# A two-block transformer kernel on one Trainium2 core: another start (idle TensorE multiplies ones, two load queues, high products first) and another order of VectorE's work in a recurrence

## The chip, the cores and the metric

The kernel runs on one core of one Trainium2 chip. The metric is the device time of one execution in microseconds (us); for the kernel before it is the median of three runs. A core has a matmul engine (TensorE, PE in the rows), a vector engine (VectorE, DVE), a scalar engine (ScalarE, ACT), a general engine (GpSimd, POOL) and SyncE (SP), which here only issues transfers. Each has a program of its own, and they meet at semaphores.

## The reference, cut to what matters

The input is 256 tokens of width 1024. Two transformer blocks are computed one after the other. The part that the change touches is the first block's beginning:

```python
h = _rmsnorm(x, norm_mix_g[l])            # x * rsqrt(mean(x^2)) * gain
z = h @ w_in[l]                           # 1024 -> hq, hf, hi, hg, fq, fk, fv, ff, mq, gates
f = lb + (1.0 - lb) * sigmoid(f_logit)    # hf
qh, kh = silu(q), 1.0 - f                 # hq
G = cumsum(log(f))                        # within a chunk of 64 tokens
A[t,s] = sum_c q[t,c] k[s,c] exp(G[t,c] - G[s,c])      # s <= t
o = A @ i + (q * exp(G)) @ S              # S is carried from chunk to chunk
```

After this recurrence come forgetting attention, attention into a memory, a gated merge, a convolutional GLU, and a second block with two SwiGLUs and differential and dilated attention.

## The kernel before

**Weights.** All weights are cut into units of up to 128 x 2048 f32 (1 MB), loaded one after the other by SP into three `raw` buffers: unit i (`load(i)`, L2023) is issued when unit i-3 has been used up (`w_lo`). Each unit is split into a high and a low part in f32r: ACT copies `raw` to `wh` (`hi_to`, L848, "high"), which may overwrite the buffer of unit i-3 only when its products are done (`unit_end`), and DVE makes `wl = raw - wh` (`lo_to`, L1245, "low"). The activations are split in the same way into `hTh` and `hTl`. A product is then three matmuls for each of eight 128-row slices: high by high, high by low, low by high (`three`, L334; all its matmuls are recorded at L340). A unit of 256 columns takes 48 matmuls of 256 columns. Units come in the order hf (0, 1), hq (2, 3), hg (4, 5), ff (6, a small one), hi (7, 8), gate (9 to 20) and so on; the number is `U[key]`. `begin(key)` on ACT or DVE is `hi_to` or `lo_to` up to two units past that key.

**The start.** x comes turned (channels on partitions) in four pieces of 128 x 512 (`XT`), interleaved on SP's queue with four pieces of unit 0, then unit 1 in two halves, units 2 and 3, then x by tokens (`X`), constants (`C`) and small tables. The norm gains `GT` (128 x 48) come on ACT's queue (L906). For each piece ACT makes the high part of x times gain (L892) and of the weights (L915), DVE the low parts (L1359, L1366), and PE then does that piece's 24 matmuls (L433), waiting for the low parts ahead of all three products. The norm itself is applied later: ACT sums the squares of `X` (L880), DVE makes the reciprocal root and writes it onto a diagonal (`norm_end`, L1299), PE multiplies ones by that diagonal after the products of hq 0 (`spread(0)`, L396, called at L452), and DVE copies the outcome to `RB` and scales hf, hq and the others with it.

**The recurrence.** DVE makes f, k and the cumulated logs G. Seven levels (half sizes 1 to 64) of decays follow: `level_sub(n)` (DVE), exponential (ACT, L962), `level_mul(n)` (DVE), `level_products(n)` (PE, L486, matmuls at L493), `level_out(n)` (DVE). They are interleaved by hand with the 12 gate units: in iteration u PE does the products of gate u and then those of level u-1; DVE does `lo_to`, scales gate u (L1335), then `level_sub(u)`, `level_out(u-1)`, `level_mul(u)` and again `lo_to`. In iteration 8 DVE runs `chunks()` (L1472): four subtractions (L1478 to L1483), the wait for ACT's exponential (L991), eight multiplications (L1488, L1489); PE's `cross_products()` (L496) needs all eight and stands behind gate 9.

```python
for u in range(12):                                  # DVE, L1507
    lo_to(U["gate", u] + (2 if u < 2 else 1))
    rows_scaled(BIGT[:, u * 512:u * 512 + 512], ("gate", u))
    ...
    if u:
        lo_to(U["gate", u] + 2)
```

Of the kernel before, what the change touches and what calls it, by code (L numbers as in the profile page):

```python
# [123 lines left out]
def build(nc, plan, I, out):  # L124
    ctx = ExitStack()
    with ctx:
# [12 lines left out]
        XT, GT = sb("XT", 2048), sb("GT", 48)  # L139
# [17 lines left out]
        def small(n):  # L157
# [8 lines left out]
        x_in, c_in, gt_in, vt_in, fb_in, lam_in, masks_in, mem_in, mt_in, gain_in, bias_in, out_st = (  # L166
            sem(n) for n in ("x_in", "c_in", "gt_in", "vt_in", "fb_in", "lam_in", "masks_in", "mem_in", "mt_in", "gain_in",
# [152 lines left out]

        def pe_program(pe):
# [108 lines left out]

            i, bs = U["hf", 0], [WF.take(), WF.take()]
            ts = [take(("hf", 0, m), bs[m]) for m in range(2)]
            for n in range(4):  # L433
                pe.wait_ge(*((w0_lo, n + 1) if n < 3 else (w_lo, 1)))
                for m in range(2):
                    ins = three(ts[m][:, 0:256], weight_left(i, 256, m * 128), right(hT_at), (2 * n, 2 * n + 1), n == 0,
                                n == 3, (lambda k: (xt_lo, k + 2)) if m == 0 else None)
                    if n == 3:
                        ins.then_inc(ps_full[bs[m]], 1)
# [3 lines left out]
            for m in range(2):  # L443
                for n, ks in enumerate((EIGHT[0:4], EIGHT[4:8])):
                    if m == 0:
                        pe.wait_ge(*((w_lo, 2) if n else (w1_lo, 1)))
                    ins = three(t[:, m * 256:m * 256 + 256], weight_left(i, 256, m * 128), right(hT_at), ks, n == 0, n == 1)
# [396 lines left out]
        def act_program(act):  # L844
# [61 lines left out]
            act.dma_start(GT[:, :], I["gains"]).then_inc(gt_in, 16)  # L906
            act.wait_ge(ones_set, 1)
            act.activation(lams, ones[:, 0:2], ACT.Copy).then_inc(*seq.next())
            act.wait_ge(gt_in, 16)
# [14 lines left out]
            squares(0, 0)  # L924
            for u in range(2):
                s = E0[:, u * 512:u * 512 + 512]
                act.wait_ge(*free(("hf", 0, 1) if u == 0 else ("hf", 1)))
                act.activation(s, s, ACT.Sigmoid).then_inc(f_sig, 1)
# [312 lines left out]
        def dve_program(dve):  # L1241
# [137 lines left out]
            rows_scaled(E0[:, 512:1024], ("hf", 1))  # L1379
            for u in range(2):  # L1380
                begin(("hq", u))
                s = Q[:, u * 512:u * 512 + 512]
                rows_scaled(s, ("hq", u))
                dve.wait_ge(q_sig, u + 1)
                dve.tensor_tensor(s, s, E1[:, u * 512:u * 512 + 512], ALU.mult).then_inc(q_made, 1)
# [86 lines left out]
            def chunks():  # L1472
# [11 lines left out]
                                  ALU.add).then_inc(ch_sub, 1)  # L1484
                dve.wait_ge(ch_exp, 1)
# [21 lines left out]
            for u in range(12):  # L1507
                lo_to(U["gate", u] + (2 if u < 2 else 1))
# [11 lines left out]
                elif u == 7:  # L1520
                    level_out(6)
                elif u == 8:
                    chunks()
                elif u == 10:
                    hgrn_sums()
                elif u == 11:
                    hgrn_scaled()
# [494 lines left out]
        def sp_program(sp):  # L2022
# [5 lines left out]
            for p in range(4):  # L2028
                c = slice(p * 512, p * 512 + 512)
                sp.dma_start(XT[:, c], I["x_turned"][:, c]).then_inc(xt_in[p], 16)  # L2030
                sp.dma_start(raw[0][:, c], I["units"][0, :, c]).then_inc(w0_in[p], 16)
# [60 lines left out]
def laid_out(inputs):  # L2092
# [24 lines left out]
    for n in range(16):  # L2117
# [3 lines left out]
    arrays = {"x": I["x"], "mem": I["mem"], "final": I["final_norm_2"], "units": units, "x_turned": turned(I["x"][0]),  # L2121
              "mem_turned": turned(I["mem"][0]), "gains": np.concatenate([as_columns(I[g][0]) for g in GAINS], 1),
# [21 lines left out]
```

## Time and profile before

| | us |
|---|---|
| median of three runs | 1017.29 (1017.09 to 1019.1) |
| the profiled execution, its own time | 1017.21 |
| span of its records | 1015.2 |
| TensorE matmul busy | 991.8 (98%) |
| VectorE busy | 667.2 (66%) |
| ScalarE busy | 484.5 (48%) |
| GpSimd busy | 74.3 (7%) |

Some 2 us of the execution's time lie outside the span. Times in rows are counted from the span's start. A matmul is pipelined: the step from one start to the next is its price in a stream, and the duration shown is longer, since the matmuls overlap. A plain f32 matmul shows as two records, an f32r one as one.

### The profile page before, as it was taken

The page shows a single profiled execution, that of the slowest core. Times are in us where ns is not written, and L with a number is a line of the kernel's source. Part 1 is how long each engine was busy: PE and PEld are TensorE (multiplying, and loading weights), DVE is VectorE, ACT ScalarE, POOL GpSimd, SP SyncE. Part 2 cuts the span into 40 slices and gives each one's busy share as a digit, 9 for nine tenths or more (in the row PEclk, how much of TensorE's full clock was granted, in tenths as well). Part 3 has the DMA queues.
Part 4 walks back from the last instruction along what each step waited for, and adds up shares of the span by engine and source line. Part 5 has one row for each costly group of instructions (what it writes and reads, how often), then busy time and mean ns, then how long its engine had stood idle before and what let it go on. Part 6 is the DMA issues. An engine that isn't in the chain of part 4 may idle for free.

```text
span 1015.2 us, 17359 instructions
## 1 busy us (share of the span) xinstructions
PE 991.8 (98%) x7468; PEld 948.6 (93%) x7468; DVE 667.2 (66%) x847; ACT 484.5 (48%) x582; POOL 74.3 (7%) x160
## 2 busy tenths in 40 slices
PE   7999999999999999999999999999999999999996
PEld 7999999899999999999899999999999999999995
DVE  5679756785776766676675555558677476555555
ACT  6554646455345545444553343435435454343433
POOL 0010112224230000000000000000002000000001
PEclk9999999999999999999999999999999999999999
DMA  9734344334356545454446454644433355555531
GB/s 344 262 132 159 129 162 167 125 126 167 125 173 238 207 179 203 161 203 163 180 169 207 167 208 167 207 166 136 156 132 122 123 185 207 184 190 174 200 125 42
DMA packets 26539, 174.37 MB, mean 172 GB/s; under 512 B 3424, under 2 KB 3808, under 8 KB 6368
## 3 DMA queue, kind: packets, MB, share of 16 engines
q1 hardware_dynamic: 25744, 170.23, 47.4%
q10 hardware_dynamic: 720, 3.04, 0.8%
q8 instruction: 59, 0.97, 0.4%
q14 instruction: 16, 0.13, 0.0%
HBM read 172.21 MB, written 1.05 MB: 171 GB/s over the span
## 4 chain that ended last, share of the span: by engine, by line
PE 88%; DVE 6%; ACT 3%; issue 2%; POOL 1%; DMA 0%; POOLq 0%; ACTq 0%; DVEq 0%
PE ps L340 81%; PE ps L576 2%; PE ps L623 2%; DVE wl L1251 2%; PE ps L389 1%; ACT wh L856 1%; PE ps L493 1%; PE ps L585 1%; DVE hTl L1359 0%; DMA GT<-in_gains 0%; DVE HG L1552 0%; POOL yTl L2002 0%; PE ps L403 0%; DVE HG L1466 0%; POOL sm L1922 0%
## 5 line engine op out<-in xcount | busy, mean ns | idle before, releaser
L340 PE MATMUL ps<-hTh,wh 128*128 128x256 f32 x1512 | 432.4, 286 | 7.5 <-DVE wl L1366 6.5
L340 PE MATMUL ps<-hTh,wl 128*128 128x256 f32 x1512 | 429.0, 284 | 0.0
L340 PE MATMUL ps<-hTl,wh 128*128 128x256 f32 x1512 | 428.8, 284 | 0.0
L1251 DVE TENSOR_TENSOR wl<-raw,wh 128x2048 fp32r<-128x2048 f32 x154 | 352.8, 2292 | 114.6 <-ACT wh L856 114.4
L856 ACT ACTIVATE wh<-raw 128x2048 fp32r<-128x2048 f32 x156 | 295.6, 1899 | 175.9 <-PE ps L340 173.6
L340 PEld LDWEIGHTS ps<-hTh,wh 128*128 128x128 f32 x1512 | 290.3, 192 | 10.1 <-DVE wl L1366 6.5
L340 PEld LDWEIGHTS ps<-hTl,wh 128*128 128x128 f32 x1512 | 290.2, 192 | 1.4
L340 PEld LDWEIGHTS ps<-hTh,wl 128*128 128x128 f32 x1512 | 290.1, 192 | 0.2
L340 PE MATMUL ps<-wh,yTh 128*128 128x512 f32 (+1 forms) x328 | 123.1, 375 | 1.3 <-issue 1.1
L340 PE MATMUL ps<-wl,yTh 128*128 128x512 f32 (+1 forms) x328 | 122.7, 374 | 0.0
L340 PE MATMUL ps<-wh,yTl 128*128 128x512 f32 (+1 forms) x328 | 122.5, 374 | 0.0
L340 PE MATMUL ps<-wh,hTh 128*128 128x256 f32 x384 | 111.5, 290 | 2.5 <-DVE wl L1251 1.3
L340 PE MATMUL ps<-wl,hTh 128*128 128x256 f32 x384 | 108.6, 283 | 0.0
L340 PE MATMUL ps<-wh,hTl 128*128 128x256 f32 x384 | 108.6, 283 | 0.0
L1335 DVE TENSOR_TENSOR PT<-ps,RB 128x512 f32<-128x512 f32 x60 | 41.5, 691 | 75.7 <-PE ps L340 68.7
L340 PEld LDWEIGHTS ps<-wh,hTh 128*128 128x128 f32 x384 | 73.4, 191 | 3.5 <-issue 1.6
L1155 ACT ACTIVATE yTh<-PT 128x512 fp32r<-128x512 f32 x33 | 20.9, 634 | 112.0 <-DVE PT L1799 112.0
L340 PEld LDWEIGHTS ps<-wl,hTh 128*128 128x128 f32 x384 | 73.6, 192 | 0.1
L340 PEld LDWEIGHTS ps<-wh,hTl 128*128 128x128 f32 x384 | 73.4, 191 | 0.0
L340 PEld LDWEIGHTS ps<-wh,yTh 128*128 128x128 f32 x328 | 62.0, 189 | 12.2 <-issue 1.6
L340 PEld LDWEIGHTS ps<-wh,yTl 128*128 128x128 f32 x328 | 61.8, 189 | 12.0
L340 PEld LDWEIGHTS ps<-wl,yTh 128*128 128x128 f32 x328 | 61.8, 189 | 10.6
(252 smaller groups left out, 804.6 us busy)
## 6 DMA issues: line engine op xcount, KB each, us to landing
raw<-in_units SPq DMA_DIRECT2D x155, 1024.0 KB, 4.9
BIGT<-in_bias ACTq DMA_DIRECT2D x1, 2048.0 KB, 7.4
XT<-in_x_turned SPq DMA_DIRECT2D x4, 256.0 KB, 5.0
raw<-in_units SPq DMA_DIRECT2D x4, 256.0 KB, 5.4
raw<-in_units SPq DMA_DIRECT2D x2, 512.0 KB, 7.3
X<-in_x SPq DMA_DIRECT2D x1, 1024.0 KB, 8.4
Hn<-in_mem SPq DMA_DIRECT2D x1, 1024.0 KB, 11.0
XT<-in_mem_turned SPq DMA_DIRECT2D x1, 1024.0 KB, 13.0
```

The source lines that it names most:

```text
L340: ins = pe.matmul(o, l(k), r(k), start=first and k == ks[0] and j == 0, stop=last and k == ks[-1] and j == 2)
L389: ins = pe.transpose(t[:, q * 128:q * 128 + 128], src[:, m * n + k * 128:m * n + k * 128 + 128], ident)
L493: ins = pe.matmul(t[:, q * 128:q * 128 + 128], s, s, start=True, stop=True)
L576: ins = pe.matmul(t[:, x:z], l, r, start=True, stop=True)
L585: ins = pe.transpose(t[:, j * 128:j * 128 + 128], P[i % 2][:, o:o + 128], ident)
L623: ins = pe.matmul(at_o(m), turned(a, i)[:, j * 128:j * 128 + 128], at_v(kb), start=x == 0, stop=x == len(js) - 1)
L856: act.activation(wh[j % NS][:, 0:n], raw[j % NR][:, 0:n], ACT.Copy).then_inc(w_hi, 1)
L1155: act.activation(yTh[:, j % 2 * 512:j % 2 * 512 + 512], g[:, :], ACT.Copy).then_inc(y_hi, 1)
L1251: dve.tensor_tensor(wl[j % NS][:, 0:n], raw[j % NR][:, 0:n], wh[j % NS][:, 0:n].bitcast(F32), ALU.subtract).then_inc(w_lo, 1)
L1335: ins = dve.tensor_tensor(o, i, by_token(2), ALU.mult)
```

## The change

1. PE first waits for `ones_set` (GpSimd's memset of a 128 x 128 tile) and does 11 f32 matmuls ones by ones of 128 columns into bank 5, whose content nobody reads.
2. `GT` and `XT` become one tile `XG`; the gains are the first 48 columns of the array with x, and the first piece is 560 columns wide. The transfer of the gains and its semaphore go.
3. Pieces 0 and 1 of unit 0 are loaded on ACT's queue, as ACT's first two instructions; SP loads x's four pieces, and pieces 2 and 3 of unit 0 between them.
4. For units 0 and 1 PE does the high by high products of a stretch when the high parts are there, and the other two kinds when the low parts are. The count of matmuls stays.
5. ACT makes the high part of unit 4 right after the squares of x, ahead of the sigmoids of hf. (The `lo_to(4)` that DVE gets stands right ahead of a `begin` that did the same.)
6. In the gate loop, iteration 1 no longer makes unit 12's low part ahead of its other work, but at its end. In iteration 8 the low part of unit 19 moves between the four subtractions and the eight multiplications of the chunks.

```diff
-        XT, GT = sb("XT", 2048), sb("GT", 48)
+        XG = sb("XG", 48 + 2048)
+        GT, XT = XG[:, 0:48], XG[:, 48:48 + 2048]
...
+        def load_piece(eng, p):
+            c = slice(p * 512, p * 512 + 512)
+            eng.dma_start(raw[0][:, c], I["units"][0, :, c]).then_inc(w0_in[p], 16)
...
+            pe.wait_ge(ones_set, 1)
+            for _ in range(11):
+                pe.matmul(bank[5][:, 0:128], ones[:, :], ones[:, :], start=True, stop=True)
             i, bs = U["hf", 0], [WF.take(), WF.take()]
             ts = [take(("hf", 0, m), bs[m]) for m in range(2)]
+
+            def high_by_high(o, m, ks, first):
+                l, r = weight_left(i, 256, m * 128)[0], right(hT_at)[0]
+                for k in ks:
+                    pe.matmul(o, l(k), r(k), start=first and k == ks[0], stop=False)
+
+            def with_low(o, m, ks, last):
+                (lh, ll), (rh, rl) = weight_left(i, 256, m * 128), right(hT_at)
+                for k in ks:
+                    pe.matmul(o, lh(k), rl(k), start=False, stop=False)
+                    ins = pe.matmul(o, ll(k), rh(k), start=False, stop=last and k == ks[-1])
+                return ins
+
             for n in range(4):
+                ks = (2 * n, 2 * n + 1)
+                pe.wait_ge(xt_hi, 2 * n + 2)
+                pe.wait_ge(*((w0_hi, n + 1) if n < 3 else (w_hi, 1)))
+                for m in range(2):
+                    high_by_high(ts[m][:, 0:256], m, ks, n == 0)
+                pe.wait_ge(xt_lo, 2 * n + 2)
                 pe.wait_ge(*((w0_lo, n + 1) if n < 3 else (w_lo, 1)))
                 for m in range(2):
-                    ins = three(ts[m][:, 0:256], weight_left(i, 256, m * 128), right(hT_at), (2 * n, 2 * n + 1), n == 0,
-                                n == 3, (lambda k: (xt_lo, k + 2)) if m == 0 else None)
+                    ins = with_low(ts[m][:, 0:256], m, ks, n == 3)
...
             for m in range(2):
+                o = t[:, m * 256:m * 256 + 256]
                 for n, ks in enumerate((EIGHT[0:4], EIGHT[4:8])):
                     if m == 0:
+                        pe.wait_ge(*((w_hi, 2) if n else (w1_hi, 1)))
+                    high_by_high(o, m, ks, n == 0)
+                    if m == 0:
                         pe.wait_ge(*((w_lo, 2) if n else (w1_lo, 1)))
-                    ins = three(t[:, m * 256:m * 256 + 256], weight_left(i, 256, m * 128), right(hT_at), ks, n == 0, n == 1)
+                    ins = with_low(o, m, ks, n == 1)
...
-            act.dma_start(GT[:, :], I["gains"]).then_inc(gt_in, 16)
+            for p in range(2):
+                load_piece(act, p)
             act.wait_ge(ones_set, 1)
             act.activation(lams, ones[:, 0:2], ACT.Copy).then_inc(*seq.next())
-            act.wait_ge(gt_in, 16)
             for p in range(4):
                 act.wait_ge(xt_in[p], 16)
                 gained_hi(p, 0, xt_hi)
...
             squares(0, 1)
             squares(0, 0)
+            hi_to(4)
             for u in range(2):
                 s = E0[:, u * 512:u * 512 + 512]
...
             rows_scaled(E0[:, 512:1024], ("hf", 1))
+            lo_to(4)
             for u in range(2):
                 begin(("hq", u))
...
-            def chunks():
+            def chunk_sub():
...
                 dve.tensor_tensor(e4[:, :, 3, :], g4[:, :, 3, :], last[2].to_broadcast([128, 4, 64]),
                                   ALU.add).then_inc(ch_sub, 1)
+
+            def chunk_mul():
                 dve.wait_ge(ch_exp, 1)
...
             for u in range(12):
-                lo_to(U["gate", u] + (2 if u < 2 else 1))
+                lo_to(U["gate", u] + (1 if u else 2))
...
                 elif u == 8:
-                    chunks()
+                    chunk_sub()
+                    lo_to(U["gate", u] + 2)
+                    chunk_mul()
...
             for p in range(4):
-                c = slice(p * 512, p * 512 + 512)
-                sp.dma_start(XT[:, c], I["x_turned"][:, c]).then_inc(xt_in[p], 16)
-                sp.dma_start(raw[0][:, c], I["units"][0, :, c]).then_inc(w0_in[p], 16)
+                c = slice(48 * (p > 0) + p * 512, 48 + p * 512 + 512)
+                sp.dma_start(XG[:, c], I["x_turned"][:, c]).then_inc(xt_in[p], 16)
+                if p > 1:
+                    load_piece(sp, p)
```

## Rows read from the trace of the kernel before

**Rows 1.** The page: the span, and busy time of TensorE with its share.
```profile
span 1015.2 us, 17359 instructions
...
PE 991.8 (98%) x7468; PEld 948.6 (93%) x7468; DVE 667.2 (66%) x847; ACT 484.5 (48%) x582; POOL 74.3 (7%) x160
```
**Rows 2.** TensorE's waits, 0 to 200 us: total us, times, longest us.
```profile
PE ps L340 <- DVE wl L1366: 6.5, 1, 6.5
PE ps L340 <- DVE wl L1251: 1.9, 3, 1.0
...
PE ps L493 <- DVE HG L1445: 1.5, 1, 1.5
```
**Rows 3.** Timeline, TensorE at the start: start us, us, engine, line, out<-in, count.
```profile
6.53 0.58 PE L340 MATMUL ps<-hTh,wh 128*128 128x256 f32 x1 [6.53 <-DVE wl L1366]
...
11.18 0.38 PE L340 MATMUL ps<-hTh,wh 128*128 128x256 f32 x1
...
12.22 0.28 PE L340 MATMUL ps<-hTh,wl 128*128 128x256 f32 x1
12.34 0.28 PE L340 MATMUL ps<-hTh,wh 128*128 128x256 f32 x1
```
**Rows 4.** Timeline, ScalarE and the split of unit 2 on VectorE, same columns.
```profile
4.33 0.91 ACT L892 ACTIVATE hTh<-XT,GT 128x256 fp32r<-128x256 f32 x2 [1.66 <-DMA GT<-in_gains]
...
17.29 2.29 DVE L1251 TENSOR_TENSOR wl<-raw,wh 128x2048 fp32r<-128x2048 f32 x1 [2.10 <-ACT wh L856]
```
**Rows 5.** Windows of 1 us: busy time of each engine, PEclk, DMA share, GB/s.
```profile
3.00:4.00 1.00, 0.00 (x0) 0.00 (x0) 0.00 (x0) 0.00 (x0) 0.00 (x0) 1.00 0.86 292
10.00:11.00 1.00, 1.00 (x7) 1.00 (x7) 0.94 (x3) 1.00 (x3) 0.00 (x0) 1.00 1.04 422
23.00:24.00 1.00, 1.00 (x11) 1.00 (x10) 0.56 (x4) 0.98 (x3) 0.60 (x2) 1.00 1.03 426
```
**Rows 6.** DMA queues, 0 to 10 us: packets, MB, share of 16 engines.
```profile
q10 hardware_dynamic: 144, 0.02, 1.9%
```
**Rows 7.** Timeline, all engines, from x's arrival to the spread of the norm.
```profile
20.65 0.63 ACT L880 ACTIVATE HG<-X 128x512 f32<-128x512 f32 x1 [0.58 <-DMA X<-in_x]
...
23.33 0.16 DVE L1286 SCALAR_TENSOR_TENSOR sm<-sm 128x2 f32<-128x2 f32 x1 [0.94 <-ACT HG L880]
...
25.54 0.48 DVE L1305 TENSOR_SCALAR diag<-C,sm 128x128 f32<-128x128 f32 x2
...
26.07 0.71 PE L403 MATMUL ps<-diag,ones 128*128 128x128 f32 x4
```
**Rows 8.** Timeline, the stretch ahead of hg 0 (ScalarE, VectorE, TensorE).
```profile
28.07 1.23 ACT L928 ACTIVATE HG<-HG 128x512 f32<-128x512 f32 x2 [3.55 <-DVE HG L1326]
29.21 1.90 ACT L856 ACTIVATE wh<-raw 128x2048 fp32r<-128x2048 f32 x1
...
31.14 2.29 DVE L1251 TENSOR_TENSOR wl<-raw,wh 128x2048 fp32r<-128x2048 f32 x1 [2.50 <-ACT wh L856]
...
33.57 0.35 PE L340 MATMUL ps<-wh,hTh 128*128 128x256 f32 x1 [1.03 <-DVE wl L1251]
```
**Rows 9.** Timeline, levels 0 and 1 of the recurrence (VectorE, TensorE).
```profile
75.77 2.28 DVE L1251 TENSOR_TENSOR wl<-raw,wh 128x2048 fp32r<-128x2048 f32 x1
...
81.62 0.68 DVE L1445 TENSOR_TENSOR HG<-HG 128x512 f32<-128x512 f32 x1
...
82.35 0.71 PE L493 MATMUL ps<-HG 128*128 128x128 f32 x4 [1.49 <-DVE HG L1445]
```
**Rows 10.** Timeline, chunks of the recurrence (VectorE, TensorE).
```profile
129.57 0.42 DVE L1483 TENSOR_TENSOR HG<-HG 128x256 f32<-128x256 f32 x1
...
132.74 2.29 DVE L1251 TENSOR_TENSOR wl<-raw,wh 128x2048 fp32r<-128x2048 f32 x1
...
133.45 1.06 PE L501 MATMUL ps<-HG 128*128 128x128 f32 x8
135.17 0.36 PE L340 MATMUL ps<-hTh,wh 128*128 128x256 f32 x1 [0.66 <-DVE wl L1251]
```

More of the change, by code:

```diff
@@ L165, in build @@
         w1_in = [sem(f"w1_in{p}") for p in range(2)]
-        x_in, c_in, gt_in, vt_in, fb_in, lam_in, masks_in, mem_in, mt_in, gain_in, bias_in, out_st = (
-            sem(n) for n in ("x_in", "c_in", "gt_in", "vt_in", "fb_in", "lam_in", "masks_in", "mem_in", "mt_in", "gain_in",
+        x_in, c_in, vt_in, fb_in, lam_in, masks_in, mem_in, mt_in, gain_in, bias_in, out_st = (
+            sem(n) for n in ("x_in", "c_in", "vt_in", "fb_in", "lam_in", "masks_in", "mem_in", "mt_in", "gain_in",
                              "bias_in", "out_st"))
@@ L2120, in laid_out @@
     lambdas = np.concatenate([I[g][0] for g in ("lambda_q1_2", "lambda_k1_2", "lambda_q2_2", "lambda_k2_2")])
-    arrays = {"x": I["x"], "mem": I["mem"], "final": I["final_norm_2"], "units": units, "x_turned": turned(I["x"][0]),
-              "mem_turned": turned(I["mem"][0]), "gains": np.concatenate([as_columns(I[g][0]) for g in GAINS], 1),
+    arrays = {"x": I["x"], "mem": I["mem"], "final": I["final_norm_2"], "units": units, "x_turned": np.concatenate([as_columns(I[g][0]) for g in GAINS] + [turned(I["x"][0])], 1),
+              "mem_turned": turned(I["mem"][0]),
               "columns": columns, "bias": bias.reshape(128, 4096), "times": log_times,
```

## The prediction

> **What bounds the kernel now.** I read the page first: TensorE is busy 991.8 of 1015.2 us [rows 1]. Nothing in the change takes away a matmul that counts, so it can only take away TensorE's idle time and its slow time, and these add up to little: the span less the busy time is 23.4 us. The list of TensorE's waits comes next [rows 2]. The first 200 us hold 6.5 us until the first operands, 1.9 us in three waits for low parts of weights, and 1.5 us ahead of the level products. All edits lie in this stretch, so everything behind 156 us can only be moved as a whole. The timeline then shows each stall's cause. At the start the first matmul comes at 6.53 us, and 22 matmuls up to 11.18 us follow at steps of 4.65/22 = 0.211 us, where the later ones step by 0.12 us [rows 3]; the granted-clock column shows 1.00 in these windows, but 256 columns in 0.211 us is the 1.2 GHz level, and 0.12 us the 2.4 GHz one. These 22 cost 22 x (0.211 - 0.12) = 2.0 us. The other stalls are 1.03 us ahead of hg 0 at 33.57 [rows 8], 1.49 us ahead of level 1's products at 82.35 [rows 9], and 0.66 us ahead of gate 10 at 135.17 [rows 10].
>
> **What really ends the start.** Two things look like the gain of the start: 6.5 us of waiting and 2.0 us of slow clock. Before believing that, look at what TensorE meets next. Behind hq 0 stands the spread of the norm, which needs the diagonal. VectorE writes it from 25.54 to 26.02, and TensorE's spread starts at 26.07 [rows 7]; the last matmul of hq 0 started at 25.90 and was not late. So the two arrive within 0.1 us of each other, and the kernel has two limits at 26 us, not one. The diagonal's chain is: X lands at 20.65, four squares, 23.33, eleven small operations, 25.54 [rows 7]. Nothing in it starts with TensorE. It starts with X's transfer, which queues behind 5.3 MB (turned x, units 0 to 3), and the transfer engines are full: share 1.04 at 422 GB/s at 10 us and 1.03 at 23 us [rows 5]. Whatever TensorE wins ahead of 26 us turns into a wait at the spread, but for (a) the 0.05 us and (b) the amount by which X itself lands earlier; call it d.
>
> **Part 1, the ones (edit 1) and high first (edit 4).** The 11 matmuls are 22 records; four such records at full clock take 26.54 - 26.07 = 0.47 us, 0.12 each (the L403 row [rows 7] and the product behind it), so at the slow pace about 0.21 each (estimate, by the ratio in rows 3): 22 x 0.21 = 4.6 us, from about 1.0 to 5.6 us. The first high parts would be there at about 5.7 us, so the ones delay nothing by more than 0.3 us. The clock rose 4.65 us after the first matmul [rows 3]; counted from 1.0 that is 5.7 us, and the real products should start at or near 2.4 GHz. High first lets TensorE start a piece about 0.7 us earlier, but each piece still ends only after its low part. Gain at the spread: 0 to 0.05. What hides it is X's chain; were that cover gone, it would be worth 2.0 us. Unit 2's low part (17.29 + 2.29 = 19.58 us [rows 4]) would stop TensorE ahead of hq 0 in any case: 19.6 + 48 x 0.12 = 25.4 us is the earliest end of hq 0.
>
> **Part 2, the transfers (edits 2 and 3).** d has three sources. The gains' queue took 1.9% of 16 engines over 10 us, 0.19 us [rows 6]; that transfer goes, for 192 bytes more a row in x's first piece. Second, the share from 3 to 4 us was 0.86 [rows 5]; the second queue can fill that spare 0.14 us, and as much again or somewhat more in each of the windows on either side, at most about 0.5 us together. Third, SP has two issues less to make, which is worth nothing once the engines are full. Against it: rows of 2 KB moved at only 292 GB/s at a share of 0.86, where longer rows reach 422 [rows 5], so share may not be what limits them; and the two first pieces now share the engines, so x's first piece can land later than now (ScalarE starts on it at 4.33, released by the gains [rows 4]), which the slack of the 26 us point covers. Bounds for d: -0.3 (x's rows now begin at an odd offset) to +0.9; I take 0.4, near the sum of the gains' 0.19 and a bit of filling. ScalarE's two issues ahead of its first work cost nothing, as it waits until 4.33 anyway.
>
> The Trainium skill says in "DMA: Bandwidth & Descriptors", section "Issuing engines are not separate DMA queues", that transfers started from several engines share the same engines and that only issue time is saved. By that rule d would be the gains' 0.19 alone and the time about 0.2 us above mine; the share of 0.86 in the trace leaves room for either.
>
> **Part 3, unit 4's high part ahead of the sigmoids (edit 5).** Now: spread 26.07, RB, hf scaled, sigmoids 28.07, high part of unit 4 29.21, low part 31.14 to 33.43, hg 0 at 33.57 [rows 8]. After: behind the squares (ended 23.1) ScalarE waits for unit 4. Behind X stand some 0.6 MB of tables and unit 4's 1.05 MB, 1.65 MB at 426 GB/s [rows 5] = 3.9 us, so it lands at about 24.6, and the high part is done at 26.5. VectorE finishes scaling hf 1 at 28.6 and does the low part until 30.9. TensorE wants it at 32.54. The 1.03 us vanish, with 1.6 us to spare. Queued behind the new wait on ScalarE are the sigmoid table load and the sigmoids, which can't start before 27.9 in any case; they would be late only if unit 4 landed after 24.8, by the difference, and nothing waits for them sooner than the q sigmoids. Next late is unit 5's low part, which moves from 38.8 to about 35.7, needed at 38.3. SP's loads that wait for low parts (units 7, 8) are issued earlier, not later. Gain 1.03 (bounds 0.5 and 1.03).
>
> **Part 4, level 1 (edit 6, first half).** From hg 1's end (45.3) to 82.35 the chain of waits runs through ScalarE and VectorE, all of it started by TensorE's hg 1, so it moves with the gains so far. In it unit 12's low part stands at 75.77, 2.28 us (2.20 to the next start), ahead of level 1 [rows 9]. Moved behind, level 1's last multiplication starts at 79.4 instead of 81.62 and ends at 80.1. TensorE is free for it at 80.86 (82.35 - 1.49). Nearly all of the 1.49 goes. What is late next: unit 12's low part itself, now 80.1 to 82.4, needed by gate 3 at 80.86 + 1.8 = 82.7. This fits with 0.3 us to spare. Unit 13's low part stays at 86.5 to 88.7 and is needed at 90.4. SP's load of unit 15 waits for unit 12's low part and goes out 4.4 us later, 8 us or more ahead of its use. Gain 1.45 (bounds 0 and 1.49).
>
> **Part 5, chunks (edit 6, second half).** Now the subtractions end at 129.99, eight multiplications at 132.8, unit 19's low part 132.74 to 135.03; TensorE does the cross products at 133.45 and then waits 0.66 us [rows 10]. After: low part 129.95 to 132.2 (under ScalarE's exponential), multiplications 132.2 to 133.9. So the wait moves ahead of the cross products: they start at 133.95 instead of 133.45, and gate 10 follows at 133.95 + 1.06 = 135.0 instead of 135.17. Gain 0.15 (bounds 0 and 0.3).
>
> **Sum**, against the profiled execution's own 1017.21 (0.08 below the median, so the same): 0.05 + 0.4 + 1.03 + 1.45 + 0.15 = 3.1 us, forecast 1014.1.
>
> **Rivals.** (A) The start counts in full: X lands early enough that the 2.0 us of slow clock show, and gain is 2.0 + 0.05 + 1.03 + 1.45 + 0.15 = 4.7, time 1012.5. For it: two queues. Against it: full transfer engines [rows 5] and 0.05 us of slack [rows 7]. (B) The wait moves on at level 1: TensorE arrives 1.45 us sooner at gate 3 and waits there for unit 12's low part. In full that gives 3.1 - 1.45, time 1015.6. For it: only 0.3 us of spare in part 4, and ScalarE's exponential between. Against: each duration in it was measured in this kernel. (C) Slower: the clock. High-first breaks TensorE's first 12 us into short bursts with waits for transfers in between, so the engine could fall back to 1.2 GHz or rise late. Real products from about 6 us at full pace reach the spread at 6 + 144 x 0.12 = 23.3, against 25.7 for the diagonal; 2.4 us of cover hold 2.4/0.091 = 26 slow matmuls. It decides the sign once 3.1 us more are lost, at 60 slow ones. If all 144 were slow: 144 x 0.091 - 2.4 - 3.1 = 7.6 us slower, 1024.8. Against it: stalls of 1.03 and 1.49 us [rows 8, 9] were followed by full pace. The Trainium skill describes exactly such a loss in "TensorE: Matmul & The Clock Gate", section "HAM oscillation — how this bites in real kernels": short bursts between transfer waits that start slow each time. By it the time would be that of C; the trace, with its two short stalls, speaks against it here. (D) The transfers of the start land later than now (d of -0.3 or below, or unit 4 late): 1014.8 to 1015.3.
>
> **How the numbers follow.** Forecast, with d from 0 to 0.9: 0.56. A 0.08; B, wholly or mostly, 0.17; C 0.07; D 0.12. A measurement of this kernel can tell 0.2% or 2.0 us from no change, so "faster" means below 1015.25: forecast, A, and nearly all of D, 0.73; "same" is B and a little of D, 0.20; slower is C, 0.07. The range holds forecast, B and D and part of A: 1012.7 to 1015.8.
>
> **What would show it.** Right: TensorE's ones from about 1.0 us, real products from about 6 us with steps of 0.12 us; a wait of 1 us or more at the spread, which starts at 25.7; no wait ahead of hg 0; level 1's products with no wait; unit 12's low part behind level 1; a wait of about 0.5 us ahead of the cross products. Wrong: a spread that starts at 24 (A), a wait at gate 3 (B), steps of 0.21 us past 8 us (C), X landing after 20.65 (D). Everything behind 156 us should be moved by one constant.

## The result and the profile after

The changed kernel takes 1015.15 us (median of 20 runs, 1014.66 to 1019.46), the kernel before 1018.0 us (20 runs, 1017.09 to 1020.9): 2.85 us less by the medians, a ratio of 0.9975 with a 95% interval of 0.9967 to 0.9983. A second series of the same kernel later gave 1015.86 us (11 runs) and 0.9982 (0.9973 to 0.9990). The forecast was 1014.1 and a range of 1012.7 to 1015.8. The times of the changed kernel fall into two groups: in the first series 13 of 20 lie between 1014.66 and 1015.48 and seven at 1016.39 or above, in the second five of 11 lie above 1016.4, which is why its median is higher.

The profiled execution of the changed kernel took 1017.18 us, 2 us more than its median, and as long as that of before. It shows both losses against the forecast: a late X, which the other profiles have too, and a fall of the clock, which most of them don't have. First TensorE's waits up to 200 us (total us, times, longest us), which answer to [rows 2]:

```profile
PE ps L606 <- DVE HG L1593: 1.8, 1, 1.8
PE ps L408 <- DVE diag L1336: 1.5, 1, 1.5
PE ps L445 <- ACT wh L945: 1.2, 1, 1.2
PE ps L438 <- POOL ones L1971: 1.0, 1, 1.0
PE ps L450 <- DVE wl L1402: 0.4, 1, 0.4
PE ps L531 <- DVE HG L1523: 0.3, 1, 0.3
PE ps L345 <- DVE wl L1282: 0.2, 1, 0.2
```

Gone are the 1.5 us ahead of level 1 and the 1.03 us ahead of hg 0. New is a wait of 1.5 us for the diagonal (L408, the spread of the norm). The first line was there before with the same 1.8 us (`PE ps L576 <- DVE HG L1557: 1.8, 1, 1.8`). The timeline of the changed kernel at the places of [rows 3, 7, 9, 10] (start us, us, engine, line, out<-in; ScalarE and TensorE):

```profile
0.98 4.60 PE L438 MATMUL ps<-ones 128*128 128x128 f32 x22 [0.98 <-POOL ones L1971]
6.78 0.71 PE L445 MATMUL ps<-hTh,wh 128*128 128x256 f32 x4 [1.19 <-ACT wh L945]
...
22.27 0.63 ACT L910 ACTIVATE HG<-X 128x512 f32<-128x512 f32 x1 [0.52 <-DMA X<-in_x]
...
25.86 0.28 PE L345 MATMUL ps<-hTh,wl 128*128 128x256 f32 x1
27.66 0.71 PE L408 MATMUL ps<-diag,ones 128*128 128x128 f32 x4 [1.52 <-DVE diag L1336]
...
33.95 0.28 PE L345 MATMUL ps<-wh,hTh 128*128 128x256 f32 x1
...
81.02 1.95 PE L523 MATMUL ps<-HG 128*128 128x128 f32 x16
...
132.58 1.13 PE L531 MATMUL ps<-HG 128*128 128x128 f32 x8 [0.34 <-DVE HG L1523]
133.47 0.36 PE L345 MATMUL ps<-hTh,wh 128*128 128x256 f32 x1
```

Read against the rows of before, this gives TensorE's lead at each point. At the spread it is 26.07 - 27.66 = -1.59 us: X was used at 22.27 instead of 20.65. At hg 0 it is 33.57 - 33.95 = -0.38, so the way from the spread to hg 0 is 1.21 us shorter. At level 1's products it is 82.35 - 81.02 = +1.33, at gate 10 135.17 - 133.47 = +1.70. That lead is still 1.69 at 178.47. Then it is gone within five microseconds. The windows of the changed kernel show why (busy time of PE, PEld, DVE, ACT, POOL, then PEclk, DMA share, GB/s):

```profile
178.00:179.00 1.00, 0.53 (x4) 0.53 (x5) 0.97 (x3) 0.00 (x0) 0.00 (x0) 1.00 1.04 442
179.00:180.00 1.00, 1.00 (x5) 0.91 (x4) 0.76 (x4) 0.00 (x0) 0.00 (x0) 0.52 0.16 66
180.00:181.00 1.00, 1.00 (x6) 1.00 (x6) 1.00 (x3) 0.62 (x3) 0.00 (x0) 0.50 0.00 0
```

Behind the 1.8 us wait (L606) the granted clock falls from 1.00 to 0.5, the 1.2 GHz level, until about 182.4 us. The second L606 group starts at 183.59 where before it started at 183.76: the lead is down to 0.17 us, so this fall cost 1.52 us. The two profiled executions end with the same span of 1015.2 us. The profile of a second execution (`again` below, 1015.57 us) has the late X (22.21) but not the fall of the clock, and its span is 1013.5 us.

### The profile page after: what moved, and what is told of

It is laid out like the page before. It is cut to its first block, busy times and chain, and to the rows that moved or that the text cites. A ratio compares the mean times of both kernels' runs of the same rounds, so it can differ in the third digit from the quotient of the medians.

```text
span 1015.2 us, 17405 instructions
## 1 busy us (share of the span) xinstructions
PE 996.6 (98%) x7490; PEld 952.3 (94%) x7490; DVE 666.8 (66%) x847; ACT 484.5 (48%) x582; POOL 74.8 (7%) x160
## 4 chain that ended last, share of the span: by engine, by line
PE 89%; DVE 5%; POOL 2%; DMA 2%; ACT 1%; issue 1%; SPq 0%; POOLq 0%; DVEq 0%; ACTq 0%
PE ps L345 82%; PE ps L606 2%; PE ps L653 2%; PE ps L523 1%; PE ps L394 1%; DVE wl L1282 1%; DMA X<-in_x 1%; PE ps L615 1%; DMA XG<-in_x_turned 1%; DVE hTl L1390 1%; POOL sm L1967 0%; DVE HG L1588 0%; POOL yTl L2038 0%; ACT HG L910 0%; PE ps L408 0%
## 5 line engine op out<-in xcount | busy, mean ns | idle before, releaser
L345 PE MATMUL ps<-hTh,wh 128*128 128x256 f32 x1480 | 421.9, 285 | 0.4 <-DVE hTl L1311 0.3
L345 PE MATMUL ps<-hTh,wl 128*128 128x256 f32 x1480 | 418.6, 283 | 0.0
L345 PE MATMUL ps<-hTl,wh 128*128 128x256 f32 x1480 | 418.5, 283 | 0.0
L345 PEld LDWEIGHTS ps<-hTh,wh 128*128 128x128 f32 x1480 | 282.8, 191 | 3.0 <-issue 1.1
L345 PEld LDWEIGHTS ps<-hTl,wh 128*128 128x128 f32 x1480 | 282.7, 191 | 1.4
L345 PEld LDWEIGHTS ps<-hTh,wl 128*128 128x128 f32 x1480 | 282.7, 191 | 0.2
L345 PE MATMUL ps<-wh,yTh 128*128 128x512 f32 (+1 forms) x328 | 123.0, 375 | 1.4 <-issue 1.1
L345 PE MATMUL ps<-wl,yTh 128*128 128x512 f32 (+1 forms) x328 | 122.6, 374 | 0.0
L345 PE MATMUL ps<-wh,yTl 128*128 128x512 f32 (+1 forms) x328 | 122.4, 373 | 0.0
L345 PE MATMUL ps<-wh,hTh 128*128 128x256 f32 x384 | 112.2, 292 | 1.5 <-DVE hTl L1301 0.9
L345 PE MATMUL ps<-wl,hTh 128*128 128x256 f32 x384 | 109.1, 284 | 0.0
L345 PE MATMUL ps<-wh,hTl 128*128 128x256 f32 x384 | 109.1, 284 | 0.0
L345 PEld LDWEIGHTS ps<-wh,hTh 128*128 128x128 f32 x384 | 74.0, 193 | 2.4 <-DVE hTl L1301 1.2
L345 PEld LDWEIGHTS ps<-wl,hTh 128*128 128x128 f32 x384 | 74.2, 193 | 0.1
L345 PEld LDWEIGHTS ps<-wh,hTl 128*128 128x128 f32 x384 | 74.1, 193 | 0.0
L345 PEld LDWEIGHTS ps<-wh,yTh 128*128 128x128 f32 x328 | 61.9, 189 | 12.3 <-issue 1.7
L345 PEld LDWEIGHTS ps<-wh,yTl 128*128 128x128 f32 x328 | 61.7, 188 | 12.0
L345 PEld LDWEIGHTS ps<-wl,yTh 128*128 128x128 f32 x328 | 61.8, 188 | 10.6
```

The costliest lines, as they stand in the source:

```text
L345: ins = pe.matmul(o, l(k), r(k), start=first and k == ks[0] and j == 0, stop=last and k == ks[-1] and j == 2)
```

## The experiments

Each is the changed kernel with one edit, unless it says otherwise. The lines of a diff are against the changed kernel. The table of all profiles stands at the end of this section. The runs come from three further series, in which the kernel before took 1017.85, 1018.02 and 1017.87 us (1018.0 in the first), so a median can be compared with one of another series to some 0.2 us.

**The changed kernel again.** No edit.

> The changed kernel unaltered, a second look at it. Theory (X's transfer sets the spread of the norm, and one execution in a few has extra losses: X 1.6 us late and a fall of the clock at 179 us): a normal execution shows X landing at 20.2 to 21.0 us, the spread of the norm at 25.6 to 26.5 us, no step of 0.21 us after 7 us, and a time of 1014.7 to 1015.3 us; against the kernel before 0.9970 to 0.9978. Rival (late X belongs to the two load queues): X lands at 22 us or later here too, the spread is at 27 us or later.

1015.86 us (11 runs). X was used at 22.21, the spread started at 27.60 behind a wait of 2.0 us. So the late X was no accident of one execution: the rival's condition (X at 22, spread at 27) is what came. All seven other profiles of a new start with X behind unit 3 have X later than the kernel before too, at 21.3 to 25.0 us, though five of them below 22. The part of the theory on normal executions fell.

**Level 1 as before.**

```diff
-                lo_to(U["gate", u] + (1 if u else 2))
+                lo_to(U["gate", u] + (2 if u < 2 else 1))
```

> The changed kernel with unit 12's low part back ahead of level 1 (iteration 1 of the gate loop as before); all else is kept. Theory: TensorE waits some 1.5 us ahead of level 1's products again, and the time is 1.3 to 1.5 us above the changed kernel's. Rival (the gain moves on to the wait for unit 12's low part at gate 3): 0 to 0.5 us above it.

1017.67 us (12 runs, ratio to before 1.0 with 0.9989 to 1.001), 1.8 us above `again` of the same series. The wait is back in full (waits of TensorE, as above):

```profile
PE ps L523 <- DVE HG L1477: 1.5, 1, 1.5
```

The theory holds, and rival B's wait for unit 12's low part at gate 3 is not in the changed kernel: none of its waits lies between 70 and 120 us. (The L345 line of 0.2 us is one at 154.56; it was there before, at 156.24.)

**Unit 4's high part behind the sigmoids.**

```diff
-            hi_to(4)
...
-            lo_to(4)
```

> The changed kernel with unit 4's high part back behind the sigmoids of hf; all else is kept. Theory: the wait ahead of hg 0 is back with 1.0 us or somewhat more, and the time is 1.0 us above the changed kernel's. Rival (the edit was of no use, since the chain behind it is set by the sigmoids): 0 to 0.3 us above it.

1016.66 us (11 runs), 0.8 us above `again`, 1.5 above the first series; its ratio to before, 0.9987 (0.9978 to 0.9996), overlaps that of `again`, so it is the profile that decides. Timeline, TensorE at hg 0:

```profile
34.33 0.36 PE L345 MATMUL ps<-wh,hTh 128*128 128x256 f32 x1 [1.04 <-DVE wl L1281]
```

The wait is back (1.03 us in [rows 8]). The theory holds in the profile. (The profiled execution, 1017.47 us, also has the fall of the clock behind the 1.8 us wait.)

**The chunks as before.**

```diff
                     chunk_sub()
-                    lo_to(U["gate", u] + 2)
                     chunk_mul()
```

> The changed kernel with unit 19's low part back behind the chunks' multiplications; all else is kept. Theory: the wait of 0.66 us ahead of gate 10 is back, the one of 0.3 to 0.5 us ahead of the cross products is gone; the time is 0.15 to 0.3 us above the changed kernel's. Rival (TensorE's wait only changed places): within 0.1 us of it.

1015.23 us (7 runs). The profile shows the exchange; TensorE at the cross products and gate 10, to be read beside the last two lines of the changed kernel's timeline above:

```profile
131.30 1.05 PE L531 MATMUL ps<-HG 128*128 128x128 f32 x8
...
133.02 0.36 PE L345 MATMUL ps<-hTh,wh 128*128 128x256 f32 x1 [0.66 <-DVE wl L1282]
```

From the cross products to gate 10 it is 133.02 - 131.30 = 1.72 us here, 133.47 - 132.58 = 0.89 in the changed kernel, where the cross products themselves wait 0.34. From level 3's products to gate 10 it is 37.64 us here and 37.31 in the changed kernel, so the exchange gives 0.33 us. The theory holds in the profile alone: the runs can't tell 0.33 us from none, and their median is 0.6 us below that of `again`, not above it.

**The old start with edits 5 and 6.** The kernel before, with `hi_to(4)` and the two moves on VectorE and nothing else.

> The kernel before with edits 5 and 6 alone (unit 4's high part early, the two moves on VectorE); the start is the old one, with no ones, one load queue, gains by themselves, three products at a time. In the profiles of the changed kernel X landed at 21.3 to 22.3 us against 20.65 before. Theory (the new start makes X land later, and so costs 0.6 to 1.6 us at the spread of the norm): X at 20.7 us, the spread at 26.1 us with no wait, time 0.6 to 1.5 us BELOW the changed kernel's, near 1014.6. Rival (the one profile of before was lucky, the start makes no difference): X at 21.3 or later here too, time within 0.3 us of the changed kernel's. Second rival (the start gains the slow clock's 2.0 us): time 1 to 2 us above the changed kernel's.

1014.74 us (5 runs), ratio 0.9967 (0.9955 to 0.998). Timeline, X's arrival, the spread and the 1.8 us wait:

```profile
20.68 0.63 ACT L880 ACTIVATE HG<-X 128x512 f32<-128x512 f32 x1 [0.59 <-DMA X<-in_x]
...
26.06 0.71 PE L403 MATMUL ps<-diag,ones 128*128 128x128 f32 x4
...
176.84 1.47 PE L576 MATMUL ps<-HG 128*128 128x128 f32 x4 [1.80 <-DVE HG L1562]
```

X and the spread are where they were before ([rows 7], 20.65 and 26.07), and the kernel without edits 1 to 4 is not slower than the changed one. Its median is the lower one by 0.4 to 1.1 us, with intervals that overlap. Edits 5 and 6 carry the gain; edits 1 to 4 carry none of it that the runs show. The last line shows how much edits 5 and 6 give by themselves: that group started at 180.16 before, so TensorE is 3.32 us ahead there. Behind it the clock of this execution fell (granted 0.50 from 177 to 180 us) and took some 1.6 us back, the reason that its own time, 1015.48 us, shows a gain of 1.73 only.

**No ones.**

```diff
-            pe.wait_ge(ones_set, 1)
-            for _ in range(11):
-                pe.matmul(bank[5][:, 0:128], ones[:, :], ones[:, :], start=True, stop=True)
```

> The changed kernel without the 11 matmuls of ones. Theory (what TensorE wins ahead of the spread turns into a wait): some 22 matmuls at steps of 0.21 us, the wait at the spread shrinks by what they cost, the time is within 0.3 us of the changed kernel's. Rival (the clock's 2.0 us count): 1.5 to 2.0 us above it.

1015.75 us (9 runs) against 1015.86 and 1015.15: no difference that the runs can tell. The first real product came at 6.65 us, the steps were 0.21 us up to 12 us, and yet the spread only waited less:

```profile
PE ps L408 <- DVE diag L1333: 0.3, 1, 0.3
```

TensorE's slow steps were paid out of the wait for the diagonal (1.5 and 2.0 us with ones, 0.3 without). The last product ahead of the spread started at 26.38 us, against 25.86 and 25.32 with ones, and the diagonal was later still. The theory holds: what TensorE wins ahead of the spread turns into a wait there.

**One load queue.**

```diff
-            for p in range(2):
-                load_piece(act, p)
...
-                if p > 1:
-                    load_piece(sp, p)
+                load_piece(sp, p)
```

> The changed kernel with all pieces of unit 0 on SP's queue, between x's pieces, as before; the gains still ride with x. Theory (the second queue is what delays x's first piece, the first low part, and with it the load of unit 3 and X behind it): ScalarE starts on x at 4.3 us instead of 5.0 to 5.3, X lands at 20.7, the time is 0.5 to 1.2 us below the changed kernel's. Rival (x's wider rows or the tables of constants delay X): X lands at 21.3 to 22.3, as in the changed kernel, and the time is within 0.3 us of it.

1015.48 us (8 runs). ScalarE started on x at 3.62 us, earlier than in any other kernel, but X was used at 21.43, late again. The theory (X at 20.7) fell: the second queue alone is not what delays X. The Trainium skill ("DMA: Bandwidth & Descriptors", section "Issuing engines are not separate DMA queues") says that a second issuing engine saves only issue time; the runs agree as far as they reach, 1015.48 against 1015.15 and 1015.86.

**Gains apart, two queues.**

```diff
-        XG = sb("XG", 48 + 2048)
-        GT, XT = XG[:, 0:48], XG[:, 48:48 + 2048]
+        XT, GT = sb("XT", 2048), sb("GT", 48)
...
+            act.dma_start(GT[:, :], I["gains"]).then_inc(gt_in, 16)
             for p in range(2):
                 load_piece(act, p)
...
+            act.wait_ge(gt_in, 16)
...
-                c = slice(48 * (p > 0) + p * 512, 48 + p * 512 + 512)
-                sp.dma_start(XG[:, c], I["x_turned"][:, c]).then_inc(xt_in[p], 16)
+                c = slice(p * 512, p * 512 + 512)
+                sp.dma_start(XT[:, c], I["x_turned"][:, c]).then_inc(xt_in[p], 16)
```

> The changed kernel with the gains in a tile and a transfer of their own again (first on ScalarE's queue, ahead of the two pieces of unit 0); x's pieces begin at even offsets as before. X landed at 20.65 and 20.68 us in the two profiles of the old start, at 21.3 to 22.3 in six profiles with gains and x in one array, one load queue or two. Theory (the shared array is what delays X, by rows that begin at a multiple of 192 bytes or by its first, wider piece): X at 20.2 to 20.9 us, the spread at 26.1 or earlier, time 0.6 to 1.2 us below the changed kernel's. Rival (the new start's order or its second queue delays X as well): X at 21.3 or later.

1016.12 us (11 runs), X at 22.66, the spread at 28.04. X did not come back to 20.65 with an array of its own, so the theory that the shared array alone delays it fell. The profile showed something else. Timeline, TensorE's first products behind the ones (which ended at 5.36 us, so that TensorE had waited 1.84 us):

```profile
7.20 0.71 PE L445 MATMUL ps<-hTh,wh 128*128 128x256 f32 x4 [1.84 <-ACT wh L947]
...
8.50 0.41 PE L450 MATMUL ps<-hTl,wh 128*128 128x256 f32 x1
8.71 0.41 PE L451 MATMUL ps<-hTh,wl 128*128 128x256 f32 x1
```

The first four products ran at the fast pace (0.71 us for four), then the step went to 0.21 us until 11.15: the clock that had risen during the ones fell again (granted 0.79 on average from 5 to 10 us). X was late in part for another reason: VectorE ended the last low part of unit 0 at 13.3 us, against 12.2 in the changed kernel and 11.84 before, and only then SP could issue unit 3 and behind it X (at 13.71). That the gains' transfer ahead of unit 0's pieces delayed them is likely and was not tried apart. Since X's issue moved too, this run doesn't clear the shared array altogether.

**Padding.** The gains' 48 columns become 128, 80 of them zeros.

```diff
-        XG = sb("XG", 48 + 2048)
-        GT, XT = XG[:, 0:48], XG[:, 48:48 + 2048]
+        XG = sb("XG", 128 + 2048)
+        GT, XT = XG[:, 0:48], XG[:, 128:128 + 2048]
...
-                c = slice(48 * (p > 0) + p * 512, 48 + p * 512 + 512)
+                c = slice(128 * (p > 0) + p * 512, 128 + p * 512 + 512)
```

> The changed kernel with the gains' 48 columns padded by 80 columns of zeros, so that x's rows begin at multiples of 512 bytes again; gains and x stay in one array, and the first piece is 640 columns wide. Theory (where rows begin is what delays X): X at 20.2 to 20.9 us. Rival (the wider first piece, or the one array): X at 21.3 us or later, time within 0.3 us of the changed kernel's.

1016.86 us (12 runs). X at 24.96, the latest of all; the profiled execution, 1019.27 us, is also the slowest of its runs. Timeline, TensorE's first products, the spread and a few products behind it:

```profile
7.00 1.19 PE L445 MATMUL ps<-hTh,wh 128*128 128x256 f32 x4 [0.95 <-ACT wh L945]
...
30.35 0.92 PE L408 MATMUL ps<-diag,ones 128*128 128x128 f32 x4 [3.35 <-DVE diag L1336]
...
31.28 0.41 PE L345 MATMUL ps<-hTl,wh 128*128 128x256 f32 x1
31.50 0.41 PE L345 MATMUL ps<-hTh,wl 128*128 128x256 f32 x1
```

Here the clock fell behind the wait at the spread itself (granted 0.50 from 31 to 34 us). And the ones had not raised it: the first four products took 1.19 us, as without ones, and the steps of 0.21 us went on until 10.2 us. Where rows begin is not what delays X.

**X ahead of unit 3.** SP's program, and the same exchange on ScalarE (`hi_to(2)` in place of `hi_to(3)` ahead of the squares) and VectorE (`lo_to(3)` behind the norm):

```diff
             load(2)
-            load(3)
             sp.dma_start(v3(X[:, :]), I["x"][0].rearrange("(t p) n -> p t n", p=128)).then_inc(x_in, 16)
             sp.dma_start(C[:, :], I["const"]).then_inc(c_in, 16)
+            load(3)
```

> The changed kernel with X and the constants loaded ahead of unit 3, whose load waits for a buffer; ScalarE does the squares ahead of unit 3's high part, VectorE the norm ahead of unit 3's low part. Theory (X's landing sets the spread): X lands near 18 us, the diagonal is there at about 23.5, and the spread starts when TensorE comes, at 25.4 to 26.1 us with no wait; the time is 0.9 to 2 us below the changed kernel's, near 1013.5. Rival (X is not what TensorE waits for; unit 3 now comes too late): a wait for unit 3's low part of 1 us or more ahead of hq 1, and no gain.

1014.38 us (5 runs, 1013.26 to 1015.08), ratio 0.9961 (0.9949 to 0.9974). Timeline, X's arrival and the spread:

```profile
17.96 0.63 ACT L910 ACTIVATE HG<-X 128x512 f32<-128x512 f32 x1 [0.65 <-DMA X<-in_x]
...
25.54 0.61 PE L408 MATMUL ps<-diag,ones 128*128 128x128 f32 x4
```

X comes 4.3 us sooner, the wait at the spread is gone, and the spread starts at 25.54, which is the limit by unit 2's low part that the prediction gave as 25.4. The theory holds in the profile; the median is 0.8 to 1.5 us lower than the changed kernel's, with intervals that overlap.

**The old start with X ahead of unit 3.** Edits 5 and 6 on the kernel before, and the exchange just shown.

> The old start (no ones, one load queue, gains apart, three products at a time) with edits 5 and 6 and with X and the constants loaded ahead of unit 3, as in the kernel whose spread started at 25.54 us. Theory (with X out of the way the new start is worth something, if little, since unit 2's low part is the next limit): the first 22 matmuls are slow, hq 0 ends when TensorE gets there, the spread starts at 26.0 to 26.1 us, and the time is about 0.5 us above that kernel's. Rival (the new start is worth its full 2.0 us once X is early): 1.5 to 2 us above it. Rival (worth nothing even then): within 0.2 us, the spread at 25.6.

1014.33 us (5 runs). Timeline, TensorE:

```profile
26.53 0.61 PE L403 MATMUL ps<-diag,ones 128*128 128x128 f32 x4
```

No wait, and 0.99 us later than 25.54: with X out of the way the new start is worth 1.0 us in the profiles (1014.28 against 1013.26 us), twice what was expected. Half of it is chance: in this execution 27 products ran at steps of 0.21 us, in that of the kernel before 22, and five more cost 5 x 0.091 = 0.46 us, which is how much later than 26.07 the spread is. The medians of five runs each (1014.33 and 1014.38) show no gain of the new start. The next kernel's median is 0.96 us below this one's, but it differs from it by the filled wait too. Nor does early X help the old start: the spread is no earlier than in `old_start` (26.06), and the medians, 1014.33 and 1014.74, can't be told apart.

**X ahead of unit 3, and the 1.8 us wait filled.** On top of the kernel with X early:

```diff
+                if (a, i) == (0, 0):
+                    for _ in range(7):
+                        pe.matmul(t[:, 0:128], ones[:, :], ones[:, :], start=True, stop=True)
```

> The changed kernel with X and the constants loaded ahead of unit 3, and with seven f32 matmuls of ones ahead of the scores of the first fox head, where TensorE waits 1.8 us. In some profiles the granted clock is 0.5 for some 3.5 us right behind this wait and TensorE loses 1.5 us; runs of all kernels fall into a lower group and one 1.5 us above. Theory (the wait brings about the fall of the clock): no fall at 180 us, and the upper group of times goes: all runs within 0.7 us, near 1013.3. Rival (the falls are not tied to that wait): the spread of the times stays, 1 us or more between the lower and the upper quarter. If the seven matmuls overran the wait, the time would be up to 0.3 us longer.

1013.37 us (5 runs, 1013.1 to 1013.47), ratio 0.9954 (0.9942 to 0.9966). Timeline, TensorE's first products, and the filled wait:

```profile
6.62 1.19 PE L445 MATMUL ps<-hTh,wh 128*128 128x256 f32 x4 [0.57 <-ACT wh L948]
...
174.35 1.73 PE L588 MATMUL ps<-ones 128*128 128x128 f32 x14
176.32 0.89 PE L609 MATMUL ps<-HG 128*128 128x128 f32 x4 [0.24 <-DVE HG L1597]
```

The seven matmuls fit into the wait, and all five runs lie within 0.37 us, where the kernel without them spread over 1.8 us and the changed kernel over 4.8 us. That is what the theory asked for, but five runs are few. The filling gains no time by itself (the group behind it starts at 176.32, at 176.23 without it); if the theory is right, only the consequence for the clock is gone. This is the fastest kernel of the study: 4.5 us below the kernel before of the same series (1017.87), 1.8 to 2.5 below the changed one. The first line shows that the ones at the start did nothing for the clock here: the products behind them stepped by 0.21 us until 10.4 us. The spread still started at 25.62.

What the profiles show of the start, in us; "used" is the start of the first square of X:

| kernel | unit 3's high part starts | X used | spread starts | waited there |
|---|---|---|---|---|
| before | 18.15 | 20.65 | 26.07 | 0 |
| old start, edits 5 and 6 | 18.17 | 20.68 | 26.06 | 0 |
| changed | 19.84 | 22.27 | 27.66 | 1.5 |
| changed, again | 19.78 | 22.21 | 27.60 | 2.0 |
| level 1 as before | 18.13 | 21.26 | 26.64 | 0.9 |
| high part 4 late | 18.97 | 21.45 | 26.83 | 0.9 |
| chunks as before | 18.61 | 21.50 | 26.88 | 0.9 |
| no ones | 19.07 | 21.61 | 26.99 | 0.3 |
| one load queue | 18.97 | 21.43 | 26.81 | 1.0 |
| gains apart | 20.15 | 22.66 | 28.04 | 1.4 |
| padded | 20.97 | 24.96 | 30.35 | 3.4 |
| X ahead of unit 3 | 21.53 | 17.96 | 25.54 | 0 |
| the same, old start | 21.18 | 17.92 | 26.53 | 0 |
| the same, new start, filled | 21.13 | 17.68 | 25.62 | 0 |

## Why the prediction was right, and where it was not

**Right, and shown.** The two limits at 26 us: the start's apparent 6.5 and 2.0 us were not to be had, since the diagonal comes from X's transfer (no ones: no difference; X early: the wait at the spread is gone). Edit 5: the wait of 1.03 us went, and came back as 1.04 when undone. Level 1: the wait of 1.49 us went (and came back when undone) with nothing given back at gate 3, though only 0.3 us were to spare. Chunks: the wait did move ahead of the cross products. Unit 4's high part ahead of the sigmoids cost nothing. Behind 156 us all moved as a whole, but for the fall of the clock. That fall comes behind a wait of 1.8 us (L576 in the kernel before, at 180.16), which the prediction left out when it listed the waits of the first 200 us.

**Mis-sized: the three terms of edits 5 and 6.** They were to give 1.03 + 1.45 + 0.15 = 2.63 us. In `again` TensorE's lead goes from -1.53 at the spread to -0.33 at hg 0, from -0.27 at level 0's products to +1.38 at level 1's, from 1.42 at level 3 to 1.75 at gate 10: 1.20 + 1.65 + 0.33 = 3.18 us. The old start with edits 5 and 6 alone agrees, with 3.32 us in all. The first two differ from the waits in the list by 0.16 to 0.17 each. A wait in the list is counted from the modelled end of the matmul before it, 0.28 us after that matmul's start, while in a stream the next one starts after 0.12. Start to start, hg 0's wait was 33.57 - 32.26 - 0.12 = 1.19 us, level 1's 82.35 - 80.58 - 0.12 = 1.65 us (32.26 and 80.58 are the last starts ahead of the two waits of [rows 8, 9]). That is the price I should have put in. For the chunks the new wait was 0.34 us where I had 0.5.

**Wrong: the step on d, the landing of X.** I took +0.4 us, with bounds of -0.3 and 0.9. Measured, by the spread: -0.6 to -1.6 us in five profiles (the changed kernel twice, and the three with a part of edits 5 and 6 undone), none inside the bounds. The direction of rival D was the true one, its size too small. What failed is the argument that full transfer engines turn each byte saved into an earlier X. They were indeed faster early on, and slower later. Windows of 2 us, from before and after (same columns as [rows 5]); before:

```profile
12.00:14.00 2.00, 2.00 (x19) 2.00 (x18) 1.26 (x2) 1.71 (x2) 0.00 (x0) 1.00 1.01 426
14.00:16.00 2.00, 2.00 (x19) 2.00 (x18) 1.19 (x1) 0.66 (x1) 0.00 (x0) 1.00 1.03 410
16.00:18.00 2.00, 2.00 (x19) 2.00 (x19) 0.71 (x1) 1.26 (x1) 0.00 (x0) 1.00 0.97 403
```

and after:

```profile
12.00:14.00 2.00, 2.00 (x18) 1.90 (x16) 1.00 (x2) 1.68 (x2) 0.00 (x0) 1.00 1.05 401
14.00:16.00 2.00, 1.62 (x13) 1.52 (x13) 1.66 (x2) 0.59 (x2) 0.00 (x0) 1.00 0.92 340
16.00:18.00 2.00, 2.00 (x19) 2.00 (x18) 0.21 (x1) 1.75 (x1) 0.00 (x0) 1.00 0.88 283
```

From 6 to 8 us the rate was 375 GB/s after and 279 before, from 16 to 18 us 283 and 403. X stands on SP's queue behind unit 3, whose issue waits for unit 0's last low part, and this came no earlier (12.2 us after, 11.84 before). I had not seen that X's issue hangs on that wait (SP issued X at 12.61 us after, at 12.24 before). What the transfers won early on was lost again: in the first 12 us they ran at 268 GB/s before and 290 after, an estimated 3.2 and 3.5 MB of the 4.2 MB (turned x and units 0 to 2) that are issued ahead of unit 3, so that around 12 us, when unit 3 went out, the faster start had only 0.7 MB in hand, against 1.0; from 12 to 20 us they ran at 411 GB/s before and 352 after. The kernels with X ahead of unit 3 have no such sag (415 and 436 GB/s in the last two windows) and X at 18 us.

**Why the number still came out.** The forecast was 3.1 us, the measured difference of medians 2.85 in the first series and 2.0 in the second. Two errors cancel in part: the terms of edits 5 and 6 were 0.55 us too small in sum, d 1.0 to 2.0 us too high. That they cancel is luck, and so is part of the hit: the 1015.15 us measured lie in the 1014.8 to 1015.3 us of rival D, which had a chance of 0.12 and whose sign, an X later than 20.65 us, is the one that came. With 3.2 us for them and a spread 0.6 to 1.6 us late the change is worth 1.6 to 2.6 us. The forecast lay in its range with the mechanism of the recurrence right and the sign of the start wrong.

**Open.** Why X is late in every new start behind unit 3. Its parts were tried one by one: with one queue it is late by 0.8 us, with the gains apart by 2.0, without ones by 1.0, with aligned rows by 4.3. SP issued X between 0.1 us earlier (12.17) and 1.5 us later (13.71) than before, by kernel, which is part of it; the sag of the rate may be the rest, and what causes the sag was not found. A smaller stock in hand at unit 3's issue is one candidate: one load queue, which had moved less by 12 us (278 GB/s), kept 391 GB/s from 14 to 18 us, where the changed kernel had 311 and the kernel before 407. But `no_level` kept 376 with the changed kernel's early rate (292), so it is not the whole of it, and it was not tried. It goes along with slow issues on SP: the lambda table took 1.2 to 1.7 us to issue in seven of these nine profiles, 0.43 to 0.50 in the old starts and with X early. The fall of the clock at the 1.8 us wait stands in 3 of the 13 profiles that have this wait (the changed kernel's, unit 4's high part late, the old start with edits 5 and 6), and not in the one that fills it; one profile is no proof, and when it comes was not found. Nor was it found why the clock rises when it does at the start: counted from TensorE's first matmul, ones or not, the slow steps went on for 3.1 to 5.8 us in 12 of the 14 profiles and for over 9 us, with a wait in between, in the other two.

## What to carry to other kernels

An idle engine at the start is no gain until one has looked for the next meeting point and who else arrives there at the same time; here X's transfer, which had cost TensorE nothing, set the end of everything won before it. Ask of that transfer not only how full the engines are but what its issue waits for: here the ungated load of X, moved ahead of a gated one on the same queue, was there 4.3 us sooner. A hand-made order on one engine can be costed to two tenths of a microsecond from the timeline (counted from start to start), as long as one checks who is next late after each move.

## What was not expected of the hardware

The clock of TensorE fell to 1.2 GHz behind single waits of 1.8 us, in some executions and not in others: at 179 us in the changed kernel (1.52 us lost), at 8 us with the gains apart, and behind 3.35 us at the spread with padding. Rival C had weighed this against waits of 1.03 and 1.49 us, which never brought it about in these profiles; nor did the wait of 2.0 us at the spread in `again`. The Trainium skill ("TensorE: Matmul & The Clock Gate", section "HAM oscillation — how this bites in real kernels") tells of such falls behind waits for transfers, of about 3 to 5 us each in its example; the runs agree in kind, but here waits of 1.8 us were enough in some executions. A part of the spread of this kernel's times, of before and after, seems to be this: with the wait filled the five runs lay within 0.37 us. Ones ahead of the first operands don't surely give them the fast clock. In seven of the ten profiles with ones it had risen when the first products came, 0.4 to 1.5 us behind the ones. With the gains apart it had risen too, but fell after four products, with 1.84 us of waiting between. And in two (`padded` and `early_filled`, with 0.95 and 0.57 us between) it had not risen at all: the products ran at 0.21 us a step until 10.2 and 10.4 us. The prediction had counted on a rise 4.65 us after the first matmul, from one profile.
